# The expert-table stage of a two-layer block, written out per head with the weights one head behind

## The reference, cut to what matters

```python
q = (hb @ w_q).reshape(128, 8, 2, 128)
sc = jnp.einsum('thcd,hcnd->thcn', q, sub_keys)          # 8 heads, 2 halves, 128 keys
s1, i1 = lax.top_k(sc[:, :, 0], 16)
s2, i2 = lax.top_k(sc[:, :, 1], 16)
cand_s = (s1[..., :, None] + s2[..., None, :]).reshape(128, 8, 256)
cand_i = (i1[..., :, None] * 128 + i2[..., None, :]).reshape(128, 8, 256)
top_s, pos = lax.top_k(cand_s, 16)
idx = jnp.take_along_axis(cand_i, pos, axis=-1)
g = jax.nn.softmax(top_s, axis=-1)
u = u_tab[idx]                                           # rows of 1024 floats
act = jax.nn.gelu(jnp.einsum('thkd,td->thk', u, hb))
v = v_tab[idx]
return jnp.einsum('thk,thkd->td', g * act, v)
```

## Time and profile before

| | us |
|---|---|
| median of 3 runs | 2569.96 (2568.51 to 2570.44) |
| span of the profiled execution | 2516.2 |
| around the span, against the median | 53.8 |
| PE busy | 2096.8 (83%) |
| DVE busy | 1009.8 (40%) |
| POOL busy | 551.6 (22%) |
| ACT busy | 529.8 (21%) |

### The profile page before, as it was taken

One profiled execution on the slowest core, in us unless ns is written; L12 is line 12 of the kernel. 1 busy time (PEld: TensorE's weight loads), 2 busy tenths in 40 slices (PEclk: granted clock), 3 DMA queues, 4 the chain that ended last, 5 costly groups with the idle time before them and its releaser, 6 DMA issues.

```text
span 2516.2 us, 27272 instructions
## 1 busy us (share of the span) xinstructions
PE 2096.8 (83%) x8874; PEld 1184.2 (47%) x8875; DVE 1009.8 (40%) x2276; ACT 529.8 (21%) x945; POOL 551.6 (22%) x560
## 2 busy tenths in 40 slices
PE   7698799867667576676798877999999999999997
PEld 6566687733223232232477664444444444444443
DVE  5885511465765756566117533121111111111113
ACT  3414410111120210111114212222222222222221
POOL 0000000177777777777100000000000000000000
PEclk9899899988878788787999988999999999999999
DMA  7275353199999999999533234699999999999995
GB/s 284 101 282 213 115 185 141 52 383 388 384 390 350 375 392 380 377 368 398 214 134 108 94 134 161 272 421 428 429 428 429 428 428 429 428 429 428 429 428 229
DMA packets 111249, 784.27 MB, mean 312 GB/s; under 512 B 12992, under 2 KB 13248, under 8 KB 79584
## 3 DMA queue, kind: packets, MB, share of 16 engines
q1 hardware_dynamic: 37472, 515.18, 49.6%
q0 software_dynamic: 73728, 268.47, 27.9%
HBM read 782.55 MB, written 1.05 MB: 311 GB/s over the span
## 4 chain that ended last, share of the span: by engine, by line
PE 45%; DVE 5%; issue 4%; POOL 2%; DMA 1%; ACT 0%; DVEq 0%; POOLq 0%; ACTq 0%
PE ps L657 39%; PE ps L806 3%; DVE arena L1719 2%; PE ps L1017 1%; POOL ring L619 1%; DMA ring<-in_peer_v,arena 1%; POOL ring L611 0%; PE ps L1048 0%; DVE arena L1643 0%; DMA ring<-in_peer_u,arena 0%; DVE arena L1727 0%; DVE arena L1646 0%; PE ps L1049 0%; DVE ps L1707 0%; DVE arena L1641 0%
## 5 line engine op out<-in xcount | busy, mean ns | idle before, releaser
L657 PE MATMUL ps<-ring,arena 128*64 128x512 f32 (+2 forms) x3328 | 743.1, 588 | 41.2 <-issue 39.8
L806 PE MATMUL ps<-ring,arena 128*128 128x512 f32 x1024 | 481.9, 634 | 222.7 <-ACT arena L1199 217.9
L657 PE MATMUL ps<-arena,ring 128*128 128x256 f32 x2272 | 521.6, 389 | 28.2 <-DVEq L1648 8.2
L657 PEld LDWEIGHTS ps<-ring,arena 128*64 128x64 f32 (+1 forms) x3328 | 259.7, 139 | 500.5 <-issue 499.2
L657 PEld LDWEIGHTS ps<-arena,ring 128*128 128x128 f32 x2272 | 439.2, 195 | 108.0 <-issue 38.1
L806 PEld LDWEIGHTS ps<-ring,arena 128*128 128x128 f32 x1024 | 207.2, 204 | 496.1 <-issue 488.8
L1626 DVE CUSTOM_DVE_ANT_0 ring<-ring,arena 128x1024 f32<-128x1024 f32 x256 | 313.5, 1225 | 221.6 <-DMA ring<-in_peer_u,arena 215.0
L1857 DVE TENSOR_TENSOR arena<-ps,arena 128x512 f32<-128x512 f32 x66 | 45.7, 692 | 651.7 <-PE ps L1017 651.7
L657 PE MATMUL ps<-arena 128*128 128x128 f32 (+5 forms) x1494 | 236.1, 317 | 84.8 <-ACT arena L1118 20.4
L611 POOL DMA_INDIRECT ring<-in_peer_u,arena x256 | 276.4, 1080 | 89.1 <-issue 73.5
L619 POOL DMA_INDIRECT ring<-in_peer_v,arena x256 | 259.1, 1012 | 79.9 <-issue 77.4
(11 more groups left out here) (292 smaller groups left out, 1062.6 us busy)
## 6 DMA issues: line engine op xcount, KB each, us to landing
ring<-in_w_exp SPq DMA_DIRECT2D x192, 2048.0 KB, 17.1
ring<-in_w_in SPq DMA_DIRECT2D x24, 2048.0 KB, 8.9
ring<-in_w_ada SPq DMA_DIRECT2D x12, 2048.0 KB, 9.3
ring<-in_w_out SPq DMA_DIRECT2D x4, 2048.0 KB, 7.7
ring<-in_w_peer_q SPq DMA_DIRECT2D x4, 2048.0 KB, 7.9
ring<-in_w_br_rnn SPq DMA_DIRECT2D x4, 1280.0 KB, 5.4
ring<-in_w_br_attn SPq DMA_DIRECT2D x2, 2048.0 KB, 7.6
ring<-in_peer_u,arena POOLq DMA_INDIRECT x256, 6.1
```

Source lines behind the costliest of these rows:

```text
L657: return pe.matmul(o, l, r, start=start, stop=stop)
L806: return pe.matmul(o, l, r, start=start, stop=False, skip_group_check=True)
```

## The change

What it does:

- All loops of the stage are written out, for 16 head-steps. `dots`, `wts`, `route_g` and `route_idx` get a place for each head, so POOL gathers from `route_idx` itself and the copy into `idx_now` goes, with its semaphore. The copy of scores (`pair_scores`) goes too.
- POOL's program is written as steps g = 0 to 16: v gathers of head g-1, then u gathers of head g. The wait for a pair's route stands at the top of the even steps, ahead of the v gathers of the odd head before.
- DVE forms the weights of head g-1 behind the third dot product (k = 2) of head g, no longer directly behind the dots of its own head.
- The search for the following pair is a generator; one piece of it (up to its next `yield`) runs behind each dot product. The softmax weights of the route (`route_weights`) are formed at k = 13 of the odd head.
- ACT and PE follow with constant waits; ACT forms the route's exponentials behind the even head's diagonals.

```diff
-            for tile in range(TT):
-                per = 2 * (2 + 2 * TOPK)
-                with pool.Fori(0, PH // 2) as i:
...
-                        pool.wait_ge(s_pv, i * (2 * TOPK) + TOPK * g + 1)
-                        own.mark(pool.wait_ge(s_route, i + tile * PH // 2 + 1))
-                        own(pool.tensor_copy(idx_now[:, par, :].bitcast(U32), route_idx[:, par, :].bitcast(U32)))
-                        pool.sem_inc(s_taken, 1)
...
+            for g in range(n_heads + 1):
+                if g < n_heads and g % 2 == 0:
+                    pool.wait_ge(s_route, g // 2 + 1)
+                if g == 1:
+                    for s in range(1, RING):
+                        pool.wait_ge(r_free[s], first_in[s])
+                if g >= 1:
+                    for k in range(TOPK):
+                        if g >= 2:
+                            pool.wait_ge(s_pv, (g - 2) * TOPK + k + 1)
+                        gather("peer_v", g - 1, k, v_gath[k], v_full[k])
+                if g < n_heads:
+                    for k in range(TOPK):
+                        n = g * TOPK + k
+                        if n >= len(u_rows):
+                            pool.wait_ge(s_dot, n - len(u_rows) + 1)
+                        gather("peer_u", g, k, u_rows[n % len(u_rows)], u_full[n % len(u_rows)])
...
-                with pe.Fori(0, PH // 2) as i:
-                    for par in range(2):
-                        g = tile * PH + par
-                        pe.wait_ge(s_diag, i * 2 + g + 1)
...
+                for g in range(tile * PH, (tile + 1) * PH):
+                    pe.wait_ge(s_diag, g + 1)
+                    for k in range(TOPK):
+                        pe.wait_ge(v_full[k], 16 * (g + 1))
+                        add(ps[:, 2 * tile, :], diag[:, g % 2, k, :], v_gath[k][:, 0:512])
+                        add(ps[:, 2 * tile + 1, :], diag[:, g % 2, k, :], v_gath[k][:, 512:D]).then_inc(s_pv, 1)
...
+                for g in range(tile * PH, (tile + 1) * PH):
+                    act.wait_ge(s_dot, TOPK * (g + 1))
+                    fn(dots[:, g, :], dots[:, g, :], ACT.Gelu_apprx_tanh).then_inc(s_act, 1)
+                    act.wait_ge(s_wts, g + 1)
+                    if g >= 2:
+                        act.wait_ge(s_pv, TOPK * (g - 1))
+                    for k in range(TOPK):
+                        last = fn(diag[:, g % 2, k, :], ident, ACT.Copy, scale=wts[:, g, k:k + 1])
+                    last.then_inc(s_diag, 1)
+                    if g % 2 == 0 and g + 2 < n_heads:
+                        act.wait_ge(s_soft_in, g // 2 + 2)
+                        fn(top_s, top_s, ACT.Exp).then_inc(s_soft, 1)
...
                     for r in range(n):
                         own.mark(dve.max(best[:, r, s], values[:, r, :]))
-                    own.settle_apart()
+                        if r % 2 == 1:
+                            yield
+                    own.settle()
                     for r in range(n):
                         own.mark(dve.max_index(where[:, r, s], best[:, r, s], values[:, r, :]))
-                    own.settle_apart()
+                        if r % 2 == 1:
+                            yield
...
-                own.mark(dve.tensor_copy(pair_scores.rearrange("p r k -> p (r k)"), flat))
...
-            dve.sem_inc(s_dot, 8)
...
+            def weigh(g):
+
+                dve.wait_ge(s_act, g + 1)
+                tt(wts[:, g, :], dots[:, g, :], route_g[:, g, :], ALU.mult).then_inc(s_wts, 1)
+
             dve.wait_ge(s_iota, 1)
...
+            for _ in route(0):
+                pass
+            route_weights(0)
+            dve.wait_ge(s_ps, n_pairs)
+            for g in range(n_heads):
+                if g % PH == 0:
+                    dve.wait_ge(s_h2r, 2 * (g // PH + 1))
+                if g % 2 == 0:
+                    ahead = route(g // 2 + 1) if g + 2 < n_heads else iter(())
+                for k in range(TOPK):
+                    n = g * TOPK + k
+                    u = n % len(u_rows)
+                    dve.wait_ge(u_full[u], 16 * (n // len(u_rows) + 1))
+                    dve.tensor_tensor_reduce(u_rows[u], u_rows[u], h2_rows[:, g // PH, :], 1.0, 0.0, ALU.mult,
+                                             ALU.add, dots[:, g, k:k + 1]).then_inc(s_dot, 1)
+                    if k == 2 and g >= 1:
+                        weigh(g - 1)
+                    next(ahead, None)
+                    if g % 2 == 1 and k == TOPK - 3 and g + 1 < n_heads:
+                        assert next(ahead, ahead) is ahead
+                        route_weights(g // 2 + 1)
+            weigh(n_heads - 1)
```

More of the change, by code:

```diff
@@ L310, in build_program @@
         qpT = carve("P", 2 * PH, T)
-        n_pairs = TT * PH // 2
-        all_scores = carve("P", (n_pairs + 1) * 4, PK)
-        pair_scores = carve("P", 4, PK)
-        scores = all_scores[:, 0:4 * n_pairs, :].rearrange("p (t r) k -> p t r k", t=TT)
+        n_heads = TT * PH
+        n_pairs = n_heads // 2
+        scores = carve("P", TT, 2 * PH, PK)
         top, top_i, top_f = (carve("P", 4, TOPK) for _ in range(3))
@@ L323, in build_program @@
         soft = carve("P", 4)
-        route_idx = carve("P", 2, TOPK)
-        route_g = carve("P", 2, TOPK)
-        idx_now = carve("P", 2, TOPK)
-        dots = carve("P", 2, TOPK)
-        wts = carve("P", 2, TOPK)
+        route_idx = carve("P", n_heads, TOPK)
+        route_g = carve("P", n_heads, TOPK)
+        dots = carve("P", n_heads, TOPK)
+        wts = carve("P", n_heads, TOPK)
         x2_rows = h2_rows
@@ L595, in _, with gather @@
             first_in = [len([n for n in range(n_first) if n % RING == s]) for s in range(RING)]
+            def gather(table, g, k, rows, loaded):
+                pool.indirect_dma_start(
+                    out=rows, out_offset=None, in_=a[table],
+                    in_offset=bass.IndirectOffsetOnAxis(ap=route_idx[:, g, k:k + 1].bitcast(U32), axis=0)
+                ).then_inc(loaded, 16)
             pool.wait_ge(r_free[0], first_in[0])
             pool.wait_ge(s_mrg, 4)
[L598 to L623 removed]
@@ L1190, in _ @@
             for tile in range(TT):
-                with act.Fori(0, PH // 2) as i:
-                    for par in range(2):
-                        g = tile * PH + par
-                        act.wait_ge(s_dots, i * 2 + g + 1)
-                        fn(dots[:, par, :], dots[:, par, :], ACT.Gelu_apprx_tanh).then_inc(s_act, 1)
-                        act.wait_ge(s_wts, i * 2 + g + 1)
-                        act.wait_ge(s_pv, i * (2 * TOPK) + TOPK * g + 1)
-                        for k in range(TOPK):
-                            last = fn(diag[:, par, k, :], ident, ACT.Copy, scale=wts[:, par, k:k + 1])
-                        last.then_inc(s_diag, 1)
-                    act.wait_ge(s_soft_in, i + tile * PH // 2 + 2)
-                    fn(top_s, top_s, ACT.Exp).then_inc(s_soft, 1)
-                act.wait_ge(s_pv, 17 + (tile + 1) * PH * TOPK)
+                for g in range(tile * PH, (tile + 1) * PH):
[10 more added lines that the diff above has]
+                        fn(top_s, top_s, ACT.Exp).then_inc(s_soft, 1)
+                act.wait_ge(s_pv, (tile + 1) * PH * TOPK)
                 for half in range(2):
@@ new lines, in top16, with of_half @@
+                        own.settle()
+            four = [P, 2, TOPK, TOPK]
+            def of_half(x, c):
+                return x.rearrange("p (h c) k -> p h c k", c=2)[:, :, c, :]
+            def route(pair):
+                per_tile = PH // 2
+                of_pair = scores[:, pair // per_tile, 4 * (pair % per_tile):4 * (pair % per_tile) + 4, :]
+                yield from top16(of_pair, top, top_i.bitcast(U32), 4)
+                own.settle()
+                own.mark(dve.tensor_copy(top_f, top_i.bitcast(U32)))
+                own.mark(tt(cand.rearrange("p h (x y) -> p h x y", y=TOPK), of_half(top, 0).unsqueeze(3).to_broadcast(four),
+                            of_half(top, 1).unsqueeze(2).to_broadcast(four), ALU.add))
+                yield
+                own.settle()
+                yield from top16(cand, top_s, pos.bitcast(U32), 2)
+                own.settle()
+                own.mark(ts(half_pos.bitcast(U32), pos.bitcast(U32), 4, None, ALU.logical_shift_right))
@@ L1460, in route @@
                 own(dve.reciprocal(soft[:, 2:4], soft[:, 2:4]))
-                own(tt(route_g, top_s, soft[:, 2:4].unsqueeze(2).to_broadcast([P, 2, TOPK]), ALU.mult))
+                own(tt(route_g[:, 2 * pair:2 * pair + 2, :], top_s,
+                       soft[:, 2:4].unsqueeze(2).to_broadcast([P, 2, TOPK]), ALU.mult))
             ada_at = {("q", 0): 0, ("q", 2): 1, ("k", 0): 2, ("k", 2): 3, ("v", 0): 4, ("v", 2): 5,
```

96 lines of the change are left out of this document (23 added, 73 removed).

## The result

The changed kernel takes 2595.19 us (median of 4 runs, 2592.65 to 2596.24), the kernel before beside it 2570.20 us (4 runs, 2568.51 to 2572.29): a ratio of 1.0113, with a 95% interval from 1.0088 to 1.0139. It is slower by 25 us. The forecast was 2623 us, with a range from 2588 to 2664.

A forecast was written before the change was run, and what follows sets the result against it. POOL, issuing one gather after the other, was taken to bound the expert-table stage at 44.24 us a head. -0.8 + 14 x 3.5 + 5.1 = +53 on the median 2569.96 gave 2623 us, range 2588 to 2664.

The forecast's parts named there:

- steps (2) and (3): Expert-table stage: loop from first u gather (S) through dots, weights, PE pass, last v gather; 47.7 us, +49 over 14 heads.
- step (4): Search in pieces between dots: POOL stalls 2 to 3.5 us a block; last v gather about S+44, hidden behind PE.
- rival B: Gathers beside spaced dots take 1.89 us, POOL late again: 50 to 51.4 us a head, +105, 2675 us; chance 0.12.
- step (3): v gathers wait for PE's pass until S+45.6; next S at 47.7; POOL's copy, stretching and DMA's rate have slack.
- Step (1): POOL's queue: gather order unchanged, copy of indices goes; leading edge gains 0.8 us, v0's start set by unchanged projections.
- step (6): Tail: last PE pass follows the one before directly, ending 72.8 us after the last u block begins, +5.1 us.
- Step (5): DVE's 512-element copy of scores (0.60 us, 8 times) goes; priced at nothing for POOL, DVE off the path.
- The 53.8 us around the span: Gap between profiled span 2516.2 us and median 2569.96 us, taken as untouched by the change.
- Rivals C and D: C: POOL stays the bound, 43.4 us a head, 2559, chance 0.08; D: no change, 2565 to 2575, chance 0.04.

The follow-up runs named there:

- e2: Changed kernel with the search run whole behind each head's last dot product, weights still one head behind: 2578.36 us, ratio 1.0258 to the kernel before.
- e9: e2 with the second of the two matmuls of each v row left out, halving PE's pass (output incomplete): 2494.57 us, ratio 0.9912 to the kernel before.
- e1: Changed kernel with a head's weights formed directly behind its own dots again, search still in pieces: 2573.17 us, ratio 1.0256 to the kernel before.
- e7: e1 with the dots' second input copied once to PSUM and read from there: 2558.81 us, ratio 0.9982 to the kernel before.
- e3: Changed kernel with the wait for all scores moved behind head 0's dots: 2574.16 us, ratio 1.0244 to the kernel before.
- e5: The kernel before, unchanged, run again on chip B: 2563.22 us, ratio 0.9998.
- e6: The changed kernel, unchanged, run again on chip B: 2597.27 us, ratio 1.0141 to the kernel before.
- e12: e10 with the dots of heads 1 to 15 reading their second input from PSUM, chip C: 2480.63 us, ratio 0.9862 to the kernel before.
- e10: Changed kernel with weights at once, search whole and score wait behind head 0's dots, chip C: 2480.47 us, ratio 0.9860 to the kernel before.

## Why the prediction was right or wrong

**Direction and place: right.** The change makes the kernel slower in the expert-table stage, in every head alike, and in the tail.

**The loop, steps (2) and (3): the loop is there, but only as a part of what sets the pace; that the number fits is in part luck.** 47.7 us a head were forecast, 47.91 measured. But the forecast filled the 3.5 us with POOL waiting for PE, and POOL waits 0.7 us a head for it; 3.5 us more go into longer gathers. The sign that the forecast named, 3 to 5 us of idle a head on PE, did not come. In 8 of 14 heads the loop closes on PE's pass, in the other six POOL is the later one. Within a head that does close there are errors that cancel. The third dot and the weights came later than its sum said: 564.38 - 553.01 = 11.4 us behind S instead of 10.2 to 10.3, since the gathers beneath the dots are stretched; so PE starts at S+16.4 and not S+15.5. The pass was 30.46 us (forecast 30.1), and the release 0.27 (599.89, the pass's end, to the last v gather at 600.16) instead of 0.9. 16.4 + 30.46 + 0.27 + 0.94 + 0.30 = 48.4, this head's time. e2 shows the loop alone, at 46.63 us a head, and e9 that PE's pass is in it.

**The second limit, step (4) and rival B: its mechanism underrated.** The step said that v's last gather would be ready at about S+44, hidden by 1 to 2 us. The distance was about right: without the lag e1 has 46.69 us a head, 1.2 less. The cause was not. It priced only POOL's stall on the u buffers, which hardly comes in the changed kernel: POOL waits for DVE 27.0 us in all, 17.2 of them once, at the ninth gather. The stretching it left to B, which had it at 50 to 51.4 us a head. Stretching is there in every block (7.20 us a head, 3.67 before), and e7 shows it to come from the dots' second SBUF input: with that input in PSUM 0.29 us a head are left. "For: dots no longer run back to back" named the right reason in B; "Against: most blocks are near 21 us" was read from blocks in which they still did. So B's mechanism is true, B's size is not, and "In it POOL's copy, its stretching and DMA's rate all have slack" in step (3) was wrong in its second term: where the stretching had slack at all, it was 1.2 us. Anyone who undid the lag alone on the strength of that sentence would gain 1.2 us a head, not 3.5.

**Step (1), the leading edge: wrong, the largest miss in the span.** It set -0.8 us; it was +16.4. The step that failed is "the unchanged projections set that": it looked at POOL's queue and not at DVE's, where a wait for all scores was moved ahead of head 0's dots. With 8 u buffers POOL stops at the ninth gather. e3 gives 17.3 us for it. The line stood in the diff, and what is queued behind that wait was not asked. Without the wait the step's sum holds: 535.85 was worked out for S1, and e3 has 536.1.

**The tail, step (6): right.** S15+72.8 was forecast and measured, +5.1.

**Step (5), the copy of scores: untested.** No run takes the copy's effect by itself. Nothing in the account (1.5 us unexplained) needs it. But the step read too much from its row. The gather at 519.71 had begun 0.59 us ahead of the copy, and the next, at 520.95, began 0.05 us behind its end; beneath none of the eight copies in the stage does a gather begin. So the row doesn't tell what a gather beneath a copy would cost, and the prediction's price of nothing was not shown.

**The 53.8 us around the span: wrong.** Only 2 us lie around a span. The kernel before takes 2513.5 to 2516 us on chips A and C and 2563 to 2570 on B and beside the result, and its first trace is, by its span, of the faster kind; that it ran on a chip of that kind is inferred. The forecast added its +53 to the median of a slower kind. Span by span it had 2569 against 2590.6, 21 us too low; the base made it 52 too high; together 30 us over the profiled run's 2592.65 (28 over the median). The range held the time because the misses had opposite signs.

This also says how to read the 1.1%. The changed kernel takes 2592 to 2597 us on all chips, the kernel before 2513.5 to 2570. Where DVE runs without stops, the change costs 3.0%, 76 us, which is what the two traces show (74.4); on the chips where DVE stops, the kernel before takes 50 us more to begin with, and the change costs 1.1 to 1.4%. So the forecast of +53 is too low for the one kind of chip and twice the measured +25 for the other. That the lagging order with pieces hides DVE's stops fits e5 and e6 (gaps 10.65 to 13.19 before, 10.79 to 11.05 after), but no run isolates it.

**Rivals C and D** did not occur in the changed kernel. The change's queue without lag and pieces does reach 41.2 us a head, under C's 43.4: of the 3.0 us against before, 0.81 is the copy of indices and 2.1 the stretching (3.67 to 1.53), whose fall no run explains. C's "PE ran 0.59 after each such idle" was shown by its rows for one pass; in four others of the same trace the granted clock in the first 6 us is 0.50 to 0.71.

## What to carry to other kernels

When a moved step makes a loop through a second engine, look for every limit within a few us of it before undoing one: here two at 46.6 and 46.7 us a head each hid the other, and only taking away both led to 41.2, where two more lie side by side. And look where the time goes even when the total is as forecast: the forecast's waits on PE were hardly there, and longer gathers had taken their place. List every wait that a diff moves, on each queue, with what stands behind it; the one that was overlooked cost 17 us. Last, set a sum against the time of the same execution: span and time of one execution lay 1.7 to 3.5 us apart in every run here, and the 53.8 us came from setting a span against other runs.

## What the runs showed of the hardware

- A gather that POOL begins beneath a dot product of 128x1024 with both inputs in SBUF (1.22 us) ends 0.81 us behind the dot's end (the median of 227 in the changed kernel's trace) and lasts up to 1.99 us instead of 0.93. With one input in PSUM the means are 948 and 941 ns, and the longest of 198 that begin beneath a dot takes 0.95 us (e7).
- Indirect gathers of 128 rows of 4 KB reach 406 to 408 GB/s at a DMA share of 1.02 to 1.03 over 500 us. With shorter issues on POOL (e12 against e10) they came no faster; they landed later instead (8.7 us behind the issue in e12, 7.9 in e10).
- One and the same kernel took 2513.5 to 2516 us on two chips and 2563 on a third. Of the 50 us between the two traces of it 39 lie in the 14 heads, nearly all as gaps of POOL, beside stops of DVE of up to 9.6 us inside a search, at nearly the same granted clock (0.920 in e5's profiled run, 0.928 in a run beside e1) and an unchanged rate of transfers where nothing held POOL (408 GB/s from 532 to 555 us in both traces). The cause stays open.
